# Delta rule of a streaming encoder layer: order of two gram products, of two masks, and the place of one row factor

## The chip, the cores and the metric

One core of one Trainium2 chip runs the whole kernel, one program from the first load to the last store. The metric is the device time of one execution in microseconds. The profile comes from one execution that was recorded on its own; its span reaches from the first to the last instruction.

## The reference, cut to what matters

One encoder layer over 2048 tokens: an input projection with a short convolution, then two groups of heads side by side (four heads of a gated delta rule, four heads of latent attention), an output projection, a feed-forward part and a per-layer embedding gate, all in float32. Only the delta rule is touched here. It works in chunks of 64 tokens:

```python
def gated_delta_rule(q, k, v, g, beta):
    ...
    decay = jnp.exp(jnp.where(tri_incl, g[..., :, None] - g[..., None, :], -jnp.inf))
    k_beta = k * beta[..., None]
    lower = jnp.where(tri_strict, jnp.einsum('nbhid,nbhjd->nbhij', k_beta, k) * decay, 0.0)
    rhs = jnp.concatenate([v * beta[..., None], k_beta * jnp.exp(g)[..., None]], -1)
    sol = lax.linalg.triangular_solve(lower + jnp.eye(CHUNK, dtype=f32), rhs,
                                      left_side=True, lower=True, unit_diagonal=True)
    u, w = sol[..., :DV], sol[..., DV:]
    attn = jnp.where(tri_incl, jnp.einsum('nbhid,nbhjd->nbhij', q, k) * decay, 0.0)
    ...
```

A scan over the chunks then carries a 128x128 state per head: `v_new = u - w S`, `o = q S + attn v_new`, `S = S exp(gl) + k^T v_new`. So `L` (called `lower` above) is the strictly lower part of the gram product of k with k, times the decay, times a factor per row (beta and the square of k's norm factor); `attn` is the gram product of q with k, times the same decay, kept up to the diagonal.

## The kernel before, in words

The function `delta_rule` treats 16 tiles of 128 tokens (two chunks each), all four heads of a tile in one [128, 4, 128] array. Each engine has its own program, and the programs meet in semaphores. They all walk through the same 19 rounds (`steps`): round r prepares tile m = r, forms the inverse's diagonal blocks of tile e = r-1, solves tile n = r-2 and advances the state with tile t = r-3. The order inside a round is written out by hand on each engine, and each engine takes its instructions strictly in that order.

**TensorE (PE)**, in a full round: `a_ws(t,0)` (L1180, w times the state), `s_z(n,0)` (transposes of U at L1151, products with L at L1153), `a_out` (L1096), `a_kv(t,0)` (L1187), `p_turn(m)` (transposes of k and q into the PSUM banks b1 and b0), `a_ws(t,1)`, `a_o(t,0)` (L1196, L1198), `s_y(n,0)` (L1160), `a_kv(t,1)`, `p_turn_v(m)` (ends with the cumulative sums into b3, L1126), `s_z(n,1)`, `a_o(t,1)`, `s_y(n,1)`, `p_gram_k(m)` (k with k into b0, L1132), `s_wu(n)` (w and u from the solved U, L1169 and L1171), `p_gram_q(m)` (k with q into b3, L1138). `p_gram_q` waits for ScalarE to have read b3 (`eg_done`, `dif_done`). Both gram products share one signal, `gram_done`, raised by the last matmul of `p_gram_q`.

**GpSimd (POOL)**, in a full round: `sums(m)` (L1031, the input of the cumulative sums), `substitute(e)` (L1039, then 28 small steps at L1047 and L1049 that invert the 16x16 blocks of L), `decayed(m)` (L1064, q times its decay), then `masks(m)`: decay times the mask up to the diagonal into `dec[:, 1]` (L1054), decay times the mask below it into `dec[:, 0]` (L1056), and that once more times the row factor `made[..., 2]` (L1059).

**VectorE (DVE)** ends a round with `s_u(n,1)` (L1462), `p_lower(m)` (L1434: L = b0 times `dec[:, 0]`, one instruction for the four heads), `p_attention(m)` (L1439: b3 times `dec[:, 1]`), `spread(e)` (L1449, puts the inverted blocks into U, which `s_z(e,0)` of the next round needs) and `a_norm(t)`. The state update `a_s` (L1480) stands earlier in the round: four instructions, one per head, each with a per-row or per-head scalar and a PSUM operand.

**ScalarE (ACT)** squares k and q, makes the decays (`eg` L1284, `dif` L1287 and L1290), copies T (L1304), scales v, squares the output, and copies w and u out of PSUM (`s_copy_wu`, L1311 and L1312). From round 16 on it also splits pieces of attention's first head (`head_high`, L1332 to L1343).

**SyncE (SP)** issues all the stage's transfers from one queue, per round: the inverted blocks to scratch memory (L968), the load of q, k, v for tile e+3 (L917), after the first has landed the blocks back in another layout (`u_blk`, L977), then after `L_done` the store of L (L980), after it has landed the four loads of its diagonal blocks (`blk`, L987), then the output's store and the load of z.

So tile m's L goes through memory to `substitute(m)` on GpSimd in the next round, and GpSimd masks the following tile only behind it.

Of the kernel before, what the change touches and what calls it, by code (L numbers as in the profile page):

```python
# [787 lines left out]
def delta_rule(nc, hT, a_log, dt_bias, norm_g, mixT, blocks_L, blocks_U, latent, at):  # L788
# [10 lines left out]
    with ExitStack() as ctx:  # L799
# [70 lines left out]
        masked = s.sem("masked")  # L870
        gram_done = s.sem("gram_done")
        L_done, attn_done = s.sem("L_done"), s.sem("attn_done")
# [41 lines left out]
        def _(sp):  # L914
# [36 lines left out]
            for r, (m, e, n, t) in enumerate(steps()):  # L951
                if r == TILES:
                    sp.wait_ge(gram_done, TILES)
                    sp.wait_ge(qd_done, TILES)
                    sp.wait_ge(turned_done, TILES)
                    sp.wait_ge(masked, 3 * TILES)
                    sp.wait_ge(L_done, TILES)
                    sp.wait_ge(attn_done, TILES)
                    for rows in (slice(0, ROPE), slice(ROPE, P)):
                        sp.dma_start(raw_kr[rows], latent["krT"]).then_inc(at.kr_loaded, 16)  # L960
                    for piece in range(5):
                        load_head(piece)
# [32 lines left out]
        def _(pool):  # L995
# [55 lines left out]
            def masks(m):  # L1051
                pool.wait_ge(dec_done, m + 1)
                reached(pool, attn_done, m)
                pool.tensor_tensor(dec[:, 1], dif[:, m % 2], each(upto[:]), ALU.mult).then_inc(masked, 1)  # L1054
                reached(pool, L_done, m)
                pool.tensor_tensor(dec[:, 0], dif[:, m % 2], each(below[:]), ALU.mult).then_inc(masked, 1)  # L1056
                pool.wait_ge(masked, 3 * m + 2)
                pool.wait_ge(made_done, 3 * (m + 1))
                pool.tensor_tensor(dec[:, 0], dec[:, 0], heads(made[:, m % 2, 2]), ALU.mult).then_inc(masked, 1)  # L1059

# [10 lines left out]
            for m, e, n, t in steps():  # L1071
                if m is not None:
                    sums(m)
                if e is not None:
                    substitute(e)
                if m is not None:
                    decayed(m)
                    masks(m)
            pool.wait_ge(at.kr_done, 2)
# [13 lines left out]
        def _(pe):  # L1093
# [35 lines left out]
            def p_gram_k(m):  # L1129
                pe.wait_ge(ssq_done, m + 1)  # L1130
                for h in range(HEADS):
                    pe.matmul(b0[:, h], qkv[:, m % 3, HEADS + h], qkv[:, m % 3, HEADS + h], start=True, stop=True)  # L1132

# [75 lines left out]
            for m, e, n, t in steps():  # L1209
# [26 lines left out]
                if first:  # L1236
                    p_gram_k(m)
                if solve:
                    s_wu(n)
                if first:  # L1240
                    p_gram_q(m)
            a_out(TILES - 1)

        @block.scalar
        def _(act):
# [35 lines left out]
            def p_decays(m):  # L1281
                act.wait_ge(turned_done, m + 1)
                reached(act, s_done, 2 * (m - 3) + 1)
                act.activation(eg[:, m % 4], b3[:], ACT.Exp).then_inc(eg_done, 1)  # L1284
                reached(act, masked, 3 * (m - 1))
                for h in range(HEADS):
# [82 lines left out]
        def _(dve):  # L1369
# [38 lines left out]
            def p_factors(m):  # L1408
# [3 lines left out]
                reached(dve, vb_done, m - 1)  # L1412
                reached(dve, masked, 3 * (m - 1))
                dve.tensor_tensor(to[:, 0], rk, rk, ALU.mult).then_inc(made_done, 1)
# [13 lines left out]
            def p_lower(m):  # L1428
                dve.wait_ge(gram_done, m + 1)
                dve.wait_ge(masked, 3 * m + 3)  # L1430
                reached(dve, L_stored, 16 * (m - 2))
                for g in range(2):
                    reached(dve, zp_done[g], NL * (m - 2))
                dve.tensor_tensor(L[:, m % 3], b0[:], dec[:, 0], ALU.mult).then_inc(L_done, 1)  # L1434

            def p_attention(m):
                dve.wait_ge(gram_done, m + 1)
                reached(dve, o_done, 2 * (m - 3))
                dve.tensor_tensor(attnT[:, m % 4], b3[:], dec[:, 1], ALU.mult).then_inc(attn_done, 1)  # L1439
# [1442 lines left out]
```

## Time and profile before

| what | value |
|---|---|
| median of 3 runs | 3335.11 us (3326.7 to 3336.2) |
| the profiled execution, its own time | 3328.85 us |
| its span, first to last instruction | 3327.4 us |
| granted TensorE clock, mean | 0.964 of full speed |
| PE busy | 3072.8 us, 92% of the span |
| DVE, ACT, POOL busy | 1593.7, 1075.9, 1077.9 us |
| the delta rule's stage | from about 666 us to about 1070 us of the span |

The profiled execution lies 6.3 us below the median of the runs, and 1.5 us of its time lie outside its span. A row of the timeline gives the start (us from the start of the span), the duration, engine, line, operation, output and inputs, how many instructions were merged, and in square brackets the idle time in front of it with what ended it. A matmul of 128 columns in float32 shows as two records, so eight records are four matmuls, one per head. SPq is SyncE's queue of transfers: its rows show when a transfer was issued, not when it landed.

### The profile page before, as it was taken

To read this page: it belongs to the slowest core of one execution; us is meant where nothing else is said; L and a number is where in the kernel's file an instruction comes from. 1 tells how busy PE (TensorE), PEld (TensorE's weight loads), DVE (VectorE), ACT (ScalarE), POOL (GpSimd) and SP (SyncE) were. 2 spreads that over 40 slices of the span, in tenths; PEclk is the share of its full clock that TensorE was granted. 3 is DMA by queue.
4 is the path that set the end of the run, shared out by engine and by line. 5 is a ranking of instruction groups with operands and counts; after the bars stand their busy time and mean duration, and the time that the engine had idled before them with its cause. 6 is when DMAs were issued, how large, how long until landed. Compare 5 with 4: busy or idle time off the path is not lost. (4 is left out here: it accounts for less than half of the span.)

```text
span 3327.4 us, 44247 instructions
## 1 busy us (share of the span) xinstructions
PE 3072.8 (92%) x15074; PEld 2540.9 (76%) x15074; DVE 1593.7 (48%) x2713; ACT 1075.9 (32%) x2399; POOL 1077.9 (32%) x1209
## 2 busy tenths in 40 slices
PE   6999997959998899989979999899998999999898
PEld 5888885648786788878768888788887788887686
DVE  3554004535664555556585455865555433233433
ACT  2211004334544555542243333433333211111321
POOL 2222241066665766410073333543331000000122
PEclk9999998979998999999989999999999999999999
DMA  3212115422324211125723222232223333233443
GB/s 136 88 75 77 76 57 168 156 76 67 82 72 107 59 52 53 67 77 178 239 69 122 91 76 83 69 117 93 77 79 110 132 98 101 91 95 117 154 123 99
DMA packets 284414, 329.18 MB, mean 99 GB/s; under 512 B 33281, under 2 KB 224641, under 8 KB 279937
## 3 DMA queue, kind: packets, MB, share of 16 engines
q1 hardware_dynamic: 238632, 265.84, 25.1%
q0 software_dynamic: 12384, 45.09, 3.8%
q10 hardware_dynamic: 33280, 16.78, 1.8%
q8 instruction: 62, 1.02, 0.1%
q14 instruction: 56, 0.45, 0.0%
HBM read 210.73 MB, written 116.92 MB: 98 GB/s over the span
## 5 line engine op out<-in xcount | busy, mean ns | idle before, releaser
L2074 PE MATMUL ff_bank<-ff_x_hi,ff_w_lo 128*128 128x512 f32 x1240 | 487.6, 393 | 31.7 <-DVE ff_w_lo L2254 22.2
L2075 PE MATMUL ff_bank<-ff_x_lo,ff_w_hi 128*128 128x512 f32 x1240 | 486.5, 392 | 0.0
L2076 PE MATMUL ff_bank<-ff_x_hi,ff_w_hi 128*128 128x512 f32 x1240 | 486.3, 392 | 0.0
L2057 POOL TENSOR_TENSOR ff_w_sum<-ff_w_raw 128x512 f32<-128x512 f32 x210 | 301.2, 1444 | 492.4 <-DVE ff_w_lo L2254 434.0
L296 PE MATMUL in_h_ps<-in_x_hi,in_w_lo 128*128 128x512 f32 x704 | 277.5, 394 | 25.7 <-POOL in_w_lo L252 25.7
L2074 PEld LDWEIGHTS ff_bank<-ff_x_hi,ff_w_lo 128*128 128x128 f32 x1240 | 235.4, 190 | 84.0 <-DVE ff_w_lo L2254 25.0
L2464 PE MATMUL fd_acc<-fd_w_hi,fd_a_lo 128*128 128x512 f32 x704 | 279.2, 397 | 11.5 <-DVE fd_a_lo L2448 11.5
L2466 PE MATMUL fd_acc<-fd_w_hi,fd_a_hi 128*128 128x512 f32 x704 | 280.4, 398 | 0.0
L2465 PE MATMUL fd_acc<-fd_w_lo,fd_a_hi 128*128 128x512 f32 x704 | 278.4, 395 | 0.0
L297 PE MATMUL in_h_ps<-in_x_lo,in_w_hi 128*128 128x512 f32 x704 | 276.8, 393 | 0.0
L298 PE MATMUL in_h_ps<-in_x_hi,in_w_hi 128*128 128x512 f32 x704 | 276.4, 393 | 0.0
L2076 PEld LDWEIGHTS ff_bank<-ff_x_hi,ff_w_hi 128*128 128x128 f32 x1240 | 235.1, 190 | 49.4
L2075 PEld LDWEIGHTS ff_bank<-ff_x_lo,ff_w_hi 128*128 128x128 f32 x1240 | 235.3, 190 | 48.8
L2153 ACT ACTIVATE ff_w_hi<-ff_w_sum 128x512 fp32r<-128x512 f32 x210 | 132.5, 631 | 286.9 <-PE ff_bank L2076 264.8
L2448 DVE TENSOR_TENSOR fd_a_lo<-fd_a_raw,fd_a_hi 128x256 fp32r<-128x256 f32 x176 | 74.5, 424 | 287.6 <-ACT fd_a_hi L2438 287.6
L2438 ACT ACTIVATE fd_a_hi<-fd_a_raw 128x256 fp32r<-128x256 f32 x176 | 73.3, 417 | 362.9 <-PE fd_acc L2466 357.3
L1652 POOL TENSOR_TENSOR at_prob<-at_prob,at_scale 128x1536 f32<-128x1536 f32 (+4 forms) x112 | 133.5, 1223 | 139.8 <-DVE at_scale L1836 133.6
L296 PEld LDWEIGHTS in_h_ps<-in_x_hi,in_w_lo 128*128 128x128 f32 x704 | 134.0, 190 | 54.5 <-issue 17.1
L2543 POOL DMA_DIRECT2D scratch_x<-fd_w_raw x16 | 8.5, 534 | 512.3 <-DVE fd_w_raw L2644 512.3
L2464 PEld LDWEIGHTS fd_acc<-fd_w_hi,fd_a_lo 128*128 128x128 f32 x704 | 132.6, 188 | 44.6 <-DVE fd_w_lo L2445 10.7
L2465 PEld LDWEIGHTS fd_acc<-fd_w_lo,fd_a_hi 128*128 128x128 f32 x704 | 132.7, 188 | 32.9
L2466 PEld LDWEIGHTS fd_acc<-fd_w_hi,fd_a_hi 128*128 128x128 f32 x704 | 132.6, 188 | 31.1
(381 smaller groups left out, 6558.5 us busy)
## 6 DMA issues: line engine op xcount, KB each, us to landing
ff_w_raw<-w_gate_up SPq DMA_DIRECT2D x44, 1024.0 KB, 5.2
scratch_hT<-in_out SPq DMA_DIRECT2D x22, 1024.0 KB, 3.9
fd_a_raw<-scratch_hid SPq DMA_DIRECT2D x176, 128.0 KB, 2.1
dr_qkv<-scratch_hT SPq DMA_DIRECT2D x16, 768.0 KB, 5.1
in_w_raw<-w_in POOLq DMA_DIRECT2D x22, 512.0 KB, 3.9
scratch_hid<-ff_first SPq DMA_DIRECT2D x44, 256.0 KB, 2.3
scratch_hid<-ff_second SPq DMA_DIRECT2D x44, 256.0 KB, 2.3
fd_w_raw<-w_down SPq DMA_DIRECT2D x22, 512.0 KB, 5.0
```

The source lines that it names most:

```text
L296: pe.matmul(acc, w_lo[:, b, ws], x_hi[:, k, ts], start=(k == 0), stop=False)
L297: pe.matmul(acc, w_hi[:, b, ws], x_lo[:, k, ts], start=False, stop=False)
L298: last = pe.matmul(acc, w_hi[:, b, ws], x_hi[:, k, ts], start=False, stop=(k == KD - 1))
L1652: last = pool.tensor_tensor(view, view, by, ALU.mult)
L2057: pool.tensor_tensor(w_sum[:, SUM_SLOT[m]], w_raw[:, b, one], w_raw[:, b, two], op).then_inc(w_sum_done, 1)
L2074: pe.matmul(acc, w_lo[:, wm, ws], x_hi[:, xm, k], start=first_mm, stop=False, skip_group_check=skip)
L2075: pe.matmul(acc, w_hi[:, wm, ws], x_lo[:, xm, k], start=False, stop=False, skip_group_check=skip)
L2076: return pe.matmul(acc, w_hi[:, wm, ws], x_hi[:, xm, k], start=False, stop=last_mm, skip_group_check=skip)
L2153: act.activation(w_hi[:, m], src, ACT.Copy).then_inc(w_hi_done, 1)
L2464: pe.matmul(to, self.a_lo[:, slot, rows], self.w_hi[:, k, cols], start=(k == k0), stop=False)
L2465: pe.matmul(to, self.a_hi[:, slot, rows], self.w_lo[:, k, cols], start=False, stop=False)
L2466: last = pe.matmul(to, self.a_hi[:, slot, rows], self.w_hi[:, k, cols], start=False, stop=(k == k1))
```

## The change

It does four things. `p_gram_q` moves on TensorE in front of `s_wu`, directly behind `p_gram_k`, and `p_gram_k` gets a signal of its own (`gram_k_done`). GpSimd does `masks` before `decayed`, within `masks` the one below the diagonal first, and no longer multiplies by the row factor. VectorE's `p_lower` waits for `gram_k_done` and the first mask alone, and brings in the row factor itself, with one instruction per head in the place of one for all four. The counts of `masked` change from three to two per tile, and the wait in `p_factors` that kept `made` from being overwritten under GpSimd goes.

```diff
@@ SyncE, before attention's first loads
-                    sp.wait_ge(masked, 3 * TILES)
+                    sp.wait_ge(masked, 2 * TILES)
@@ GpSimd
             def masks(m):
                 pool.wait_ge(dec_done, m + 1)
+                reached(pool, L_done, m)
+                pool.tensor_tensor(dec[:, 0], dif[:, m % 2], each(below[:]), ALU.mult).then_inc(masked, 1)
                 reached(pool, attn_done, m)
                 pool.tensor_tensor(dec[:, 1], dif[:, m % 2], each(upto[:]), ALU.mult).then_inc(masked, 1)
-                reached(pool, L_done, m)
-                pool.tensor_tensor(dec[:, 0], dif[:, m % 2], each(below[:]), ALU.mult).then_inc(masked, 1)
-                pool.wait_ge(masked, 3 * m + 2)
-                pool.wait_ge(made_done, 3 * (m + 1))
-                pool.tensor_tensor(dec[:, 0], dec[:, 0], heads(made[:, m % 2, 2]), ALU.mult).then_inc(masked, 1)
...
                 if m is not None:
+                    masks(m)
                     decayed(m)
-                    masks(m)
@@ TensorE
                 for h in range(HEADS):
-                    pe.matmul(b0[:, h], qkv[:, m % 3, HEADS + h], qkv[:, m % 3, HEADS + h], start=True, stop=True)
+                    last = pe.matmul(b0[:, h], qkv[:, m % 3, HEADS + h], qkv[:, m % 3, HEADS + h], start=True, stop=True)
+                last.then_inc(gram_k_done, 1)
...
                 if first:
                     p_gram_k(m)
+                    p_gram_q(m)
                 if solve:
                     s_wu(n)
-                if first:
-                    p_gram_q(m)
@@ ScalarE
-                reached(act, masked, 3 * (m - 1))
+                reached(act, masked, 2 * (m - 1))
@@ VectorE
                 reached(dve, vb_done, m - 1)
-                reached(dve, masked, 3 * (m - 1))
...
             def p_lower(m):
-                dve.wait_ge(gram_done, m + 1)
-                dve.wait_ge(masked, 3 * m + 3)
+                dve.wait_ge(gram_k_done, m + 1)
+                dve.wait_ge(masked, 2 * m + 1)
...
-                dve.tensor_tensor(L[:, m % 3], b0[:], dec[:, 0], ALU.mult).then_inc(L_done, 1)
+                for h in range(HEADS):
+                    op = dve.scalar_tensor_tensor(L[:, m % 3, h], b0[:, h], made[:, m % 2, 2, h:h + 1], dec[:, 0, h],
+                                                  ALU.mult, ALU.mult)
+                op.then_inc(L_done, 1)
 
             def p_attention(m):
                 dve.wait_ge(gram_done, m + 1)
+                dve.wait_ge(masked, 2 * m + 2)
```

## Rows read from the trace of the kernel before

**Rows 1.** The page's first part: busy time, share of the span, instructions by engine.
```profile
PE 3072.8 (92%) x15074; PEld 2540.9 (76%) x15074; DVE 1593.7 (48%) x2713; ACT 1075.9 (32%) x2399; POOL 1077.9 (32%) x1209
```

**Rows 2.** Windows between `p_gram_q` starts: length, busy PE, PEld, DVE, ACT, POOL, clock, DMA.
```profile
751.30:771.95 20.65, 19.49 (x157) 16.92 (x155) 13.10 (x38) 10.45 (x46) 11.24 (x32) 1.00 0.12 29
...
815.51:840.04 24.53, 22.50 (x156) 19.60 (x155) 13.76 (x38) 10.49 (x47) 16.95 (x37) 0.86 0.35 95
...
860.69:881.48 20.79, 19.50 (x157) 16.92 (x156) 12.88 (x38) 10.50 (x47) 13.95 (x35) 1.00 0.29 77
...
sum 258.88, PE 239.83 PEld 208.53 DVE 157.25 ACT 125.90 POOL 166.56; mean PE 19.99 PEld 17.38 DVE 13.10 ACT 10.49 POOL 13.88
```

**Rows 3.** Timeline of PE, one round's end, 858 to 864 us.
```profile
858.01 1.06 PE L1132 MATMUL dr_b<-dr_qkv 128*128 128x128 f32 x8
858.90 0.61 PE L1169 MATMUL dr_b<-dr_U,dr_kbg 128*128 128x128 f32 x4
...
860.69 1.06 PE L1138 MATMUL dr_b<-dr_qkv 128*128 128x128 f32 x8
861.68 1.09 PE L1180 MATMUL dr_b<-dr_S,dr_wT 128*64 128x128 f32 x8
863.87 0.44 PE L1151 MATMUL dr_b<-dr_ident,dr_U 128*128 128x128 f32 x2 [1.10 <-DVE dr_U L1449]
```

**Rows 4.** Timeline of POOL in the same round, from the end of `substitute` on.
```profile
857.00 1.26 POOL L1064 TENSOR_TENSOR dr_qdT<-dr_qkv,dr_eg 128x512 f32<-128x512 f32 x1
...
859.46 1.25 POOL L1056 TENSOR_TENSOR dr_dec<-dr_dif,dr_below 128x512 f32<-128x512 f32 x1
860.79 1.04 POOL L1059 TENSOR_TENSOR dr_dec<-dr_dec,dr_made 128x512 f32<-128x512 f32 x1
...
867.39 0.84 POOL L1039 TENSOR_TENSOR dr_inv<-dr_ident_b,dr_blk 32x256 f32<-32x256 f32 x1 [4.55 <-DMA dr_blk<-scratch_blocks_L]
```

**Rows 5.** Timeline of DVE, 852 to 864 us.
```profile
852.32 1.12 DVE L1480 SCALAR_TENSOR_TENSOR dr_S<-dr_S,dr_eg,dr_b 128x128 f32<-128x128 f32 x4 [0.67 <-PE dr_b L1187]
...
861.92 0.69 DVE L1434 TENSOR_TENSOR dr_L<-dr_b,dr_dec 128x512 f32<-128x512 f32 x1 [3.29 <-POOL dr_dec L1059]
...
863.13 0.68 DVE L1449 TENSOR_TENSOR dr_U<-dr_u_blk,dr_diag 128x512 f32<-128x512 f32 x1
```

**Rows 6.** Timeline of SP's queue in the same round.
```profile
857.51 0.37 SPq L917 DMA_DIRECT2D dr_qkv<-scratch_hT  x1
858.55 0.36 SPq L977 DMA_DIRECT2D dr_u_blk<-scratch_blocks_U  x1
862.64 0.34 SPq L980 DMA_DIRECT2D scratch_blocks_L<-dr_L  x1
```

**Rows 7.** DMA view of the stage: transfers by line, KB each, median us to landing.
```profile
dr_qkv<-scratch_hT SPq DMA_DIRECT2D x16, 768.0 KB, 5.1
...
scratch_blocks_L<-dr_L SPq DMA_DIRECT2D x16, 256.0 KB, 2.0
...
dr_u_blk<-scratch_blocks_U SPq DMA_DIRECT2D x16, 32.0 KB, 4.2
```

**Rows 8.** Timeline of PE, rounds 17 to 18: no gram product stands behind `s_wu`.
```profile
1047.75 0.68 PE L1169 MATMUL dr_b<-dr_U,dr_kbg 128*128 128x128 f32 x4 [0.16 <-DVE dr_U L1462]
...
1049.80 1.37 PE L1180 MATMUL dr_b<-dr_S,dr_wT 128*64 128x128 f32 x8
1051.11 0.66 PE L1096 MATMUL dr_b<-dr_ident,dr_on 128*128 128x128 f32 x4
```

**Rows 9.** Timeline of PE, the start of `s_z` in rounds 3, 7 and 17.
```profile
730.71 0.69 PE L1151 MATMUL dr_b<-dr_ident,dr_U 128*128 128x128 f32 x2 [4.93 <-DVE dr_U L1449]
...
819.55 0.44 PE L1151 MATMUL dr_b<-dr_ident,dr_U 128*128 128x128 f32 x2 [1.96 <-DVE dr_U L1449]
...
1032.34 0.69 PE L1151 MATMUL dr_b<-dr_ident,dr_U 128*128 128x128 f32 x2 [1.75 <-DVE dr_U L1449]
```

**Rows 10.** Timeline of ACT in round 17: the copy of T behind attention's pieces.
```profile
1034.70 0.89 ACT L1304 ACTIVATE dr_T<-dr_b 128x256 f32<-128x256 f32 x2
```

More of the change, by code:

```diff
@@ L870, in delta_rule @@
         masked = s.sem("masked")
-        gram_done = s.sem("gram_done")
+        gram_k_done, gram_done = s.sem("gram_k_done"), s.sem("gram_done")
         L_done, attn_done = s.sem("L_done"), s.sem("attn_done")
```

## Prediction, made before the changed kernel ran

> **What bounds the kernel now.** PE is busy 92% of the span [rows 1], but this is a mean over stages; only the delta rule's stage changes, so I read that stage alone, first by windows from one `p_gram_q` to the next [rows 2]. Tiles 3 to 15 are twelve such rounds in 258.88 us, 21.57 us each. The undisturbed ones last 20.65 us and hold 19.49 us of PE work, so PE idles only 1.16 us in them. Three of the twelve are longer with a granted clock under 1.00; the worst is the one of 24.53 us at 0.86, with 22.50 us of PE.
>
> Next the timelines, for who holds whom. PE's last idle time in a round ends on DVE's `spread` [rows 3], which in DVE's order stands behind L and attention. L waits 3.29 us for POOL's row factor [rows 5], which is POOL's fourth operation after the substitution [rows 4]. L is stored 0.03 us after it is made [rows 6], and the substitution of the next round starts at 867.39, 4.78 us after L's end at 862.61 [rows 4, 5]. So there is a **loop**: substitution (10.4 us: the next one ends about 877.75, the one before started 20.77 us before the 867.39) – three masks and q's decay (4.8 us) – L (0.7 us) – memory (4.8 us), 20.7 us together. PE's own round has a floor of 20.65 us in today's order, since L needs `gram_done` from the last product of the round. Two loops of nearly equal length take turns, and where both are late PE waits near 2 us, as the 1.96 us ahead of the slowest round's `s_z` [rows 9].
>
> **The change part by part.** I count time E from the substitution's end (857.00 in the round shown) and G from `p_gram_k`'s start (858.01).
>
> *POOL.* Before L it now has one mask, 1.26 us, in the place of four operations up to 861.83, that is 4.83 us [rows 4]. The row factor's 1.04 us go; q's decay, the mask up to the diagonal and the next `sums` (3.5 us) fall into the 4.78 us in which POOL waits for memory. Cost nothing, cover 4.8 us plus L; if that cover went, 3.5 us would return to the loop.
>
> *DVE.* L becomes four `scalar_tensor_tensor` of 128x128 with one PSUM operand. No row shows exactly these operands. Nearest is the state update, same form and size: 1.12 us for four, against 0.69 us for today's single one [rows 5]. I take +0.43 us; the lower bound is 0, the upper +0.7 (four separate 0.34 us). In POOL's loop this counts in full.
>
> *POOL's loop, new:* 10.4 + 1.26 + 0.1 + 1.12 + 4.78 = 17.7 us, if L's transfer takes what it takes today.
>
> *PE.* `p_gram_q` (0.99 us) goes ahead of `s_wu`. Its two waits are on ScalarE work that ended before the first gram product: today `p_gram_k` to `a_ws` runs without a gap. What was behind it is now uncovered: `a_ws` needs w and u copied, and these copies used to run under `p_gram_q`. Rounds 17 to 18 show that order: from the start of `s_wu` to the end of `a_ws` 1051.11 - 1047.75 = 3.36 us [rows 8]. Today the same work takes 858.90 to 862.77 (863.87 less the 1.10 idle) less 0.99, 2.88 us [rows 3]; 0.07 us of the difference is its first load. So **+0.41 us** per round. Bounds: 0 and 0.6.
>
> *The wait for `spread`.* In G: the gram products end at 1.88, L starts about 1.05 and ends 2.17, attention 2.85, `spread` 3.5; `a_ws` ends 0.99 + 0.89 + 3.29 = 5.2 and `s_z` finds U ready. The 0.96 us that even a PE-bound round idles here (20.65 less 19.49, less 0.2 that the state update causes) go. `spread` also needs `u_blk`, which lands about 5.1 to 5.7 after E (issued 1.55 after it, median 4.2 to landing) [rows 6, 7]; with POOL's loop ahead, E lies near G - 2.8, so it lands at 2.9, in time. Next late is nothing outside PE: the round becomes 20.65 - 0.96 + 0.41 = **20.10 us**, and POOL's 17.7 follows it. Twelve rounds: 258.88 - 241.2 = **17.7 us**. Some 6 us of these are the slowed matmuls of three rounds (PE busy 239.83 against 12 x 19.49 = 233.9 [rows 2]); the slowest of them begins with that wait of 1.96 us [rows 9], and I take it that without such waits the clock stays at 2.4 GHz.
>
> *The fill.* Up to round 3 the POOL loop alone decides (4.93 us of idle PE [rows 9]). Round 0: L moves by 4.83 - 1.0 (no q decay in front there) less 1.26 and 0.43, about 1.9 us. In round 1 one is tempted to take 3.1 us more, but L's store is then issued 2.5 us after E, and the 768 KB load of q, k, v was issued 0.5 us after E and needs 5.1 us [rows 6, 7]. The row that shows what happens to a transfer behind it is `u_blk`: 32 KB, 4.2 us, while L's 256 KB with nothing in front take 2.0 us [rows 7]. So L's store lands about E + 6.3 instead of E + 7.7: 1.35 us. `spread` in round 2 comes 1.0 us sooner after its E (it now waits for `u_blk`, not for L). 1.9 + 1.35 + 1.0 = **4.2 us**. By the Trainium skill (DMA: Bandwidth & Descriptors, "Two DMAs through the same engine are not ordered"), descriptors of one queue on one DMA engine begin in order though they may finish otherwise. That agrees with the 4.2 us. Without such an order the fill would give some 6 us.
>
> *The drain.* Round 16 opens with the gain at `s_z` of 0.96 - 0.41, 0.5 us. In round 17 PE waited 1.75 us for `spread` [rows 9]; this goes, but T's copy starts at 1034.70 only, behind attention's pieces on ACT [rows 10], and the state update stands behind Z in DVE's order. I take 1.0 us.
>
> **Sum.** 4.2 + 17.7 + 0.5 + 1.0 = 23.4 us off 3328.85 (the profiled execution's own time), 3305.4. The median of the runs lies 6.3 us higher; against it I give **3312 us**.
>
> **The rivals.**
>
> *A. PE's round is not the only bound; less comes.* If `u_blk` (behind the load) or L's store slips, L's wait persists in part. L's store is now issued G + 2.2, about E + 5.0, just as the load and `u_blk` clear. Two more us there and POOL's loop is 19.7, still under PE; 3 more and it is 20.7. Then the rounds give 12 x (21.57 - 20.7) = 10, with the rest 13 us: 3322. If only the slowed matmuls are saved, 6 + 4, 3325. For: the 4.2 us of [rows 7]. Against: 2.4 us of slack. Chance 0.20.
>
> *B. More comes.* If the copies hide after all (no 0.41), 12 x 0.41 = 5 us more, and if round 3 no longer starts at the low clock (its idle time shrinks from 4.9 to about 3.4), 3 us more: 3304. For: matmuls at L1151 take 0.69 us there against 0.44 [rows 3, 9]. Against: rows 8 show the copies uncovered. Chance 0.17.
>
> *C. Slower.* L's store collides with the load in every round. From L's end to the substitution's start 4.78 us pass, 2.0 of them the store [rows 4, 5, 7], so with a store of x us POOL's loop is 15.7 + x. It decides against today's 21.57 when x passes 5.9 us. At x = 7, as when it queued behind the whole load and its own reading, the round is 22.7: 12 x 1.1 = 14 us slower less the fill's 4, 3345. Against: PE holds L back to E + 5, when the load has landed. Chance 0.04.
>
> *D. It does nothing.* The stage ends on attention's pieces on POOL and ACT instead of on the rounds, so that the rounds' gain is waited away. Against: those pieces stand behind the last rounds' ACT work and shift with it. 3335. Chance 0.04.
>
> **How the numbers follow.** Forecast 0.55. A measurement of this kernel can tell about 0.3% from no change, 10 us: faster means below 3325. Faster: 0.54 of the forecast, B's 0.17 and 0.09 of A, 0.80. Same: 0.01 of the forecast, 0.10 of A, D's 0.04, 0.15. Slower: C's 0.04 and 0.01 of A, 0.05. The bounds of the unknown costs (0 to 0.7 on L, harmless with 2.4 us of slack; 0 to 0.6 on PE, +5 to -2 us; 0 to 3 us of clock in round 3) carry the forecast from 3303 to 3318. The range takes in most of A and B: 3300 to 3325.
>
> **What the profile after would show.** Right: windows between `p_gram_k` starts near 20.1 us with clock 1.00 in all; no idle time before L1151 ended by `spread` in full rounds; about 0.2 us before `a_ws` and again inside it; L's four instructions start within 0.2 us of `p_gram_k`'s end and take 1.1 us; POOL waits for `blk` and then again for ACT's decays (L1290) before its first mask. Wrong: DVE's L still waiting for `dec` in full rounds (A or C: then look at the store of L's landing, 2.0 us before); rounds of 19.7 (B); a clock under 1.00 in the middle rounds; a stage that starts attention as late as before (D).

## Result and profile after the change

| | before | changed |
|---|---|---|
| median of runs | 3324.6 us (7 runs, 3321.8 to 3336.2) | 3310.57 us (7 runs, 3303.6 to 3314.5) |
| ratio, 95% interval | | 0.9946 [0.9928, 0.9964] |
| the profiled execution | 3328.85 us | 3312.63 us |
| its span, mean granted clock | 3327.4 us, 0.964 | 3311.2 us, 0.964 |

The change is faster by more than the 0.3% named in the prediction: by the ratio some 18 us, by the two medians 14, by the two profiled executions 16.2. The median shown ahead of the prediction, 3335.11, was that of three runs; the four later runs of the same kernel lie between 3321.8 and 3324.6. The forecast of 23.4 us off 3335 is a ratio of 0.993, at the favourable end of the interval. That the forecast time of 3312 us lies only 1.4 us from the measured 3310.57 is luck: the base was 10.5 us too high, and the gain, by the medians, 9.4 us too large.

I read the stage in the same pieces as before. The windows of the changed kernel, cut at the starts of `p_gram_q` from tile 3 on (length, busy PE, PEld, DVE, ACT, POOL, clock, DMA share, GB/s), answer to [rows 2]:

```profile
743.70:763.55 19.85, 19.49 (x156) 16.86 (x155) 13.55 (x41) 10.49 (x48) 12.95 (x34) 1.00 0.12 33
...
823.23:843.87 20.64, 19.75 (x157) 16.89 (x155) 13.53 (x41) 10.50 (x48) 12.94 (x34) 1.00 0.32 83
843.87:864.59 20.72, 19.74 (x156) 16.89 (x155) 13.36 (x41) 10.49 (x48) 13.88 (x35) 1.00 0.32 88
864.59:884.45 19.86, 19.54 (x156) 16.87 (x155) 13.42 (x41) 10.49 (x48) 12.93 (x34) 1.00 0.33 89
...
sum 240.41, PE 235.16 PEld 202.50 DVE 162.51 ACT 125.91 POOL 155.34; mean PE 19.60 PEld 16.87 DVE 13.54 ACT 10.49 POOL 12.94
```

Twelve rounds now take 240.4 us where they took 258.9, none has a clock under 1.00, and PE is busy 235.2 us of them where it was busy 239.8: 4.7 us of the 18.5, mostly matmuls that no longer run at half rate; the rest is idle time of PE. Nine rounds last 19.85 to 19.97 us, one 20.20 and two over 20.6.

The stage in three pieces, from DVE's first clearing of S to attention's first score product:

| piece | before | changed | difference | forecast |
|---|---|---|---|---|
| start to `p_gram_k` of tile 3 (fill) | 82.31 | 78.51 | -3.8 | -4.2 |
| `p_gram_k` of tile 3 to that of tile 15 | 258.88 | 240.42 | -18.5 | -17.7 |
| from there to attention (drain) | 63.13 | 69.95 | **+6.8** | -1.5 |
| whole stage | 404.32 | 388.88 | -15.4 | -23.4 |

(The stage also began 2.0 us sooner in this profile and what follows it took 1.2 us longer; both lie outside the edit.) Two pieces come out as worked out, against this one profile of the kernel before. A second profile of the same rounds exists: `e8_before_pieces_behind_t`, described below, is the kernel before with an edit that lies behind them. Its twelve rounds take 255.0 us, so the rounds' gain is 18.5 by one profile and 14.6 by the other. The third piece has the other sign, and the experiments had to explain it.

The timeline of PE in the changed kernel shows the new order and the price of the copies, beside [rows 3]:

```profile
863.70 1.06 PE L1129 MATMUL dr_b<-dr_qkv 128*128 128x128 f32 x8
864.59 1.06 PE L1136 MATMUL dr_b<-dr_qkv 128*128 128x128 f32 x8
865.49 0.61 PE L1167 MATMUL dr_b<-dr_U,dr_kbg 128*128 128x128 f32 x4
...
867.46 1.37 PE L1178 MATMUL dr_b<-dr_S,dr_wT 128*64 128x128 f32 x8
868.77 0.44 PE L1149 MATMUL dr_b<-dr_ident,dr_U 128*128 128x128 f32 x2
```

Both gram products stand together, and from the start of `s_wu` (L1167) to the end of `a_ws` (L1178) pass 3.28 us. The `s_z` behind it has no idle time in brackets: U was ready.

The timeline of DVE in two rounds of the changed kernel answers to [rows 5]:

```profile
848.03 0.69 DVE L1449 TENSOR_TENSOR dr_U<-dr_u_blk,dr_diag 128x512 f32<-128x512 f32 x1 [2.23 <-DMA dr_u_blk<-scratch_blocks_U]
...
884.65 1.13 DVE L1431 SCALAR_TENSOR_TENSOR dr_L<-dr_b,dr_made,dr_dec 128x128 f32<-128x128 f32 x4 [0.47 <-PE dr_b L1129]
885.70 0.68 DVE L1439 TENSOR_TENSOR dr_attnT<-dr_b,dr_dec 128x512 f32<-128x512 f32 x1
887.26 0.69 DVE L1449 TENSOR_TENSOR dr_U<-dr_u_blk,dr_diag 128x512 f32<-128x512 f32 x1 [0.89 <-DMA dr_u_blk<-scratch_blocks_U]
```

L now waits for its gram product (0.47 us of idle DVE) and no longer 3.29 us for POOL. `spread` (L1449), which I had expected to find its block landed, waits for it in ten of the twelve rounds, 0.6 to 2.2 us. Most of this wait is covered, since PE comes for U later than that; at 2.1 and 2.2 us it is not, and these are the two rounds over 20.6 us, in which PE idles 0.57 and 0.66 us ahead of `s_z`.

The timeline of POOL in the changed kernel, from the end of one substitution to the start of the next, answers to [rows 4]:

```profile
881.67 1.27 POOL L1054 TENSOR_TENSOR dr_dec<-dr_dif,dr_below 128x512 f32<-128x512 f32 x1
882.89 1.28 POOL L1056 TENSOR_TENSOR dr_dec<-dr_dif,dr_upto 128x512 f32<-128x512 f32 x1
884.13 1.28 POOL L1061 TENSOR_TENSOR dr_qdT<-dr_qkv,dr_eg 128x512 f32<-128x512 f32 x1
885.35 1.05 POOL L1031 TENSOR_TENSOR dr_cums<-dr_upto,dr_scal 128x512 f32<-128x512 f32 x1
891.72 0.84 POOL L1039 TENSOR_TENSOR dr_inv<-dr_ident_b,dr_blk 32x256 f32<-32x256 f32 x1 [5.32 <-DMA dr_blk<-scratch_blocks_L]
```

The mask that L needs ends at 882.94, before L's product does; the other three operations lie in the time in which POOL would wait for memory, and 5.32 us of waiting are left over. POOL no longer sets the pace. One term of its loop grew, though: from L's end to the start of the next substitution 4.7 to 7.1 us pass in the twelve rounds, where it was 4.8 to 5.7 before; in the round shown it is 891.72 - 885.78 = 5.94.

### The profile page after: what moved, and what is told of

It reads as the page before. It is cut to its first block and busy times, and to the rows that moved or that the text cites. A ratio compares the mean times of both kernels' runs of the same rounds, so it can differ in the third digit from the quotient of the medians.

```text
span 3311.2 us, 44267 instructions
## 1 busy us (share of the span) xinstructions
PE 3075.2 (93%) x15074; PEld 2541.1 (77%) x15074; DVE 1600.0 (48%) x2761; ACT 1075.6 (32%) x2399; POOL 1061.2 (32%) x1193
```

## Experiments

Every time is the median of its runs, every ratio is against runs of the kernel before on the same chip. "Rounds" is the sum of the twelve windows, "drain" the third piece of the table above.

**The changed kernel twice more**, unaltered, on two chips.

> The changed kernel, unaltered, once more, as the yardstick for the others. Theory T (two loops set the rounds; the drain gives some 7 us back through a late T copy on ScalarE and low clock behind it): 0.9946 of before within 0.003; the twelve windows between second gram products sum to 240 to 243 us; in round 17 PE idles 2.7 us before its second w-times-state product and the clock is at 1.2 GHz behind it. Rival R (the low clock of the drain is chance, not a wait): round 17 shows the same order of work, but PE at 2.4 GHz, and the stage is 6 to 8 us shorter than the 388.9 us of the first profile.

> The changed kernel a third time, beside the others on the same chip. Windows 240 to 243 us; ratio 0.993 to 0.996; the drain 66 to 70 us if its low clock has a cause in the order of work (a wait of 2 to 2.8 us before the second w-times-state product of round 17), 62 to 64 in this draw if it is chance.

Measured: 3311.81 us, 0.9944 [0.9921, 0.9966], and 3307.57 us, 0.9941 [0.9921, 0.996]. Fill 78.5 and 78.6, rounds 240.7 and 239.8: all but the same. The drain is not: 67.4 us in one and 61.1 in the other, after 70.0 in the first profile. The timeline of PE in the drain, first profile of the changed kernel:

```profile
1005.91 0.44 PE L1149 MATMUL dr_b<-dr_ident,dr_U 128*128 128x128 f32 x2 [0.39 <-DVE dr_U L1449]
...
1011.87 0.76 PE L1178 MATMUL dr_b<-dr_S,dr_wT 128*64 128x128 f32 x5 [2.75 <-DVE dr_S L1480]
...
1026.11 0.68 PE L1167 MATMUL dr_b<-dr_U,dr_kbg 128*128 128x128 f32 x4 [0.16 <-DVE dr_U L1462]
...
1032.68 0.76 PE L1178 MATMUL dr_b<-dr_S,dr_wT 128*64 128x128 f32 x5 [1.22 <-DVE dr_S L1480]
...
1047.39 1.11 PE L1093 MATMUL dr_b<-dr_ident,dr_on 128*128 128x128 f32 x4 [4.83 <-DVE dr_on L1496]
```

and the same rows in the third profile (`c2_change_third`):

```profile
1007.56 0.44 PE L1149 MATMUL dr_b<-dr_ident,dr_U 128*128 128x128 f32 x2 [1.47 <-DVE dr_U L1449]
...
1012.44 0.76 PE L1178 MATMUL dr_b<-dr_S,dr_wT 128*64 128x128 f32 x5 [1.67 <-DVE dr_S L1480]
...
1021.96 0.68 PE L1167 MATMUL dr_b<-dr_U,dr_kbg 128*128 128x128 f32 x4 [0.16 <-DVE dr_U L1462]
...
1028.53 0.76 PE L1178 MATMUL dr_b<-dr_S,dr_wT 128*64 128x128 f32 x5 [1.22 <-DVE dr_S L1480]
...
1039.07 1.12 PE L1093 MATMUL dr_b<-dr_ident,dr_on 128*128 128x128 f32 x4 [4.83 <-DVE dr_on L1496]
```

Round 17's two waits sum to 3.14 us in both (0.39 + 2.75, 1.47 + 1.67; in the second profile 1.05 + 2.08). The same work from the state update to the next `s_wu` then takes 14.24 us in one and 9.52 in the other, and the last stretch 14.71 and 10.54. These 4.7 and 4.2 us are the whole 8.9 between the drains, and the windows view over ten of these microseconds says what they are. In the first profile:

```profile
1012.00:1022.00 10.00, 10.00 (x52) 8.89 (x51) 3.83 (x9) 0.98 (x3) 7.61 (x6) 0.55 0.76 203
```

The same window in the third profile, `c2_change_third`:

```profile
1012.00:1022.00 10.00, 9.41 (x77) 8.20 (x77) 5.22 (x14) 3.16 (x11) 8.19 (x6) 1.00 0.90 245
```

At a granted clock of 0.55 PE gets through 52 matmuls in the time in which it gets through 77 at 1.00. So the +6.8 us of the drain is TensorE at 1.2 GHz, in some executions of one and the same program and not in others; with 2.4 GHz through rounds 17 and 18 the drain is 61.1 us, 2.0 less than before.

**TensorE's order alone**, on the kernel before:

```diff
                 if first:
                     p_gram_k(m)
+                    p_gram_q(m)
                 if solve:
                     s_wu(n)
-                if first:
-                    p_gram_q(m)
```

> The kernel before with one edit: the k-with-q product ahead of w and u on TensorE. GpSimd and VectorE as before. Theory T: L gets its gram product 1.8 us sooner but still waits for GpSimd's row factor, so GpSimd's loop of 20.7 us sets every round: windows near 20.75 us, sum 248 to 251 against 258.9 before and 240.4 after; time 6 to 10 us below before (ratio 0.997 to 0.998). Rival (TensorE's order alone is what paid): sum 240 to 243, ratio 0.995.

Measured: 3328.89 us, 1.0001 [0.9991, 1.0012]; rounds 262.0. By itself the new order brings nothing. Windows of this kernel:

```profile
809.36:837.15 27.79, 23.82 (x157) 20.65 (x156) 13.97 (x38) 10.61 (x48) 18.62 (x41) 0.82 0.34 92
```

and its PE timeline inside that window:

```profile
817.37 0.69 PE L1151 MATMUL dr_b<-dr_ident,dr_U 128*128 128x128 f32 x2 [3.77 <-DVE dr_U L1448]
817.85 1.06 PE L1153 MATMUL dr_b<-dr_U,dr_L 128*128 128x128 f32 x4
```

PE can now do a round in 19.85 us while POOL's loop still needs 20.7. PE runs ahead for three rounds (19.85, 20.15, 20.82), is then held 3.77 us (3.88 and 2.84 the next two times), and its products behind that wait take 1.06 us for four, where they take 0.61 at full clock. That costs what the order gives. My expected 248 to 251 us had no place for this: an engine that is faster than its supplier pays the difference in lumps, and the lumps are long enough to go with a lower clock.

**GpSimd's and VectorE's part alone**: the changed kernel with `p_gram_q` put back behind `s_wu`, the diff above the other way round.

> The changed kernel with the k-with-q product put back behind w and u on TensorE; GpSimd, VectorE and the separate signal stay. Theory T: L comes early and GpSimd's loop is short, but attention and behind it spread wait for the last product, so TensorE idles 0.96 us before each round's solve: windows 20.65 us, sum 247 to 250; time 8 to 13 us below before (ratio 0.996 to 0.9975). Rival (GpSimd's loop alone is what paid): sum 240 to 243, ratio 0.995.

Measured: 3309.6 us, 0.994 [0.9924, 0.9957], no different from the whole change. Every round lasts 20.05 us, not the 20.65 that I expected, and they sum to 240.6. PE's timeline has the reason:

```profile
863.78 0.44 PE L1149 MATMUL dr_b<-dr_ident,dr_U 128*128 128x128 f32 x2 [0.37 <-DVE dr_U L1450]
```

The wait ahead of `s_z` shrinks from 0.96 to 0.37 us. I had taken it to go only with the product's move, because attention and `spread` stand behind `gram_done`. But `spread` stood behind L too, and L, with `gram_k_done` of its own, is now made under `s_wu`; only attention's 0.69 us still come between the last product and `spread`. So moving the product is worth 0.2 us a round in the quiet rounds (20.05 against 19.86), 2.3 us in twelve, and the three long rounds give it back: nothing that the profiles of the rounds or the times can tell. Its drain, 73.6 us, is longer than any of the changed kernel's: in round 17 PE waits 2.64 us for `spread`, and some 15 us at 1.2 GHz follow. The gain is in POOL's order, L's own signal, or both.

**The row factor back on POOL**, directly behind the mask below the diagonal, L again a single operation, the rest of the change kept:

```diff
+                pool.tensor_tensor(dec[:, 0], dec[:, 0], heads(made[:, m % 2, 2]), ALU.mult).then_inc(masked, 1)
...
-                for h in range(HEADS):
-                    op = dve.scalar_tensor_tensor(L[:, m % 3, h], b0[:, h], made[:, m % 2, 2, h:h + 1], dec[:, 0, h],
-                                                  ALU.mult, ALU.mult)
-                op.then_inc(L_done, 1)
+                dve.tensor_tensor(L[:, m % 3], b0[:], dec[:, 0], ALU.mult).then_inc(L_done, 1)
```

> The changed kernel with the row factor back on GpSimd, right behind the mask below the diagonal (L is again one VectorE instruction for four heads). Theory T: GpSimd's loop grows from 17.7 to 18.4 us, still under TensorE's 19.85, so the windows stay at 19.85 to 20.2 us, sum 240 to 243; only the fill loses 0.6 us in each of its rounds, 2 us in all; ratio to before 0.994 to 0.996. Rival (the row factor's move carried the gain): windows above 20.5 us, sum over 246.

> The changed kernel with the row factor on GpSimd, unaltered, once more. Theory T: its windows sum to 238 to 241 us again; its ratio is that of the changed kernel within the interval (0.993 to 0.996), since the drain of 62.5 us in its first profile was one draw of 62 to 70. Rival (its drain is short for a reason): drain again under 64 us and ratio under 0.9935.

Measured: 3306.12 us, 0.9937 [0.9921, 0.9954], and again 3303.80, 0.9938 [0.9916, 0.996]; rounds 238.4 and 238.6, drain 62.5 and 62.4. It is as fast as the change, perhaps 4 to 6 us faster, which the intervals can't tell. The full rounds have slack for POOL's 1.04 us; moving them to DVE brings nothing there. In both profiles the rounds are even 1.2 to 2.4 us shorter than in the three of the change, with no wait of PE ahead of `s_z` in a full round; why was not tested. The fill, 78.8 and 78.6 us against 78.5, lost 0.1 to 0.3 us and not the 2 that I expected. The product's move and the factor's move can each be taken back alone without loss; both at once was not tried. What is left to carry the gain is that the mask for L comes first on POOL and that L has a signal of its own.

**Attention's first pieces behind T's copy** in the drain, because in the first profile ACT spends 1004.85 to 1009.64 on them while the copy of T, Z and the state update wait behind:

```diff
-        HIGH_AT = {(TILES, "wu"): (0, 2), (TILES + 1, "t"): (2, 5), (TILES + 1, "wu"): (5, 11), (TILES + 2, "end"): (11, PIECES)}
+        HIGH_AT = {(TILES + 1, "t"): (0, 5), (TILES + 1, "wu"): (5, 11), (TILES + 2, "end"): (11, PIECES)}
...
-                if (r, place) == (TILES, "wu"):
+                if (r, place) == (TILES + 1, "t"):
```

> The changed kernel with ScalarE's splitting of attention's rope key and first two pieces moved from the end of round 16 to behind round 17's copies of T. Theory T (the late T copy holds Z, and behind it the state update in VectorE's order; the low clock follows that wait): TensorE's idle time before the second w-times-state product of round 17 falls from 2.75 to 1.2 us, the clock stays at 2.4 GHz until the last round, and from the last k-with-k product to attention's first matmul it takes 61 to 64 us instead of 70.0 and 67.4; time 4 to 7 us below the changed kernel (ratio to before 0.992 to 0.9935). Rival (the low clock of the drain comes of itself, or of the 1.2 us waits that are in every drain round): the wait shrinks, the clock still falls, the drain stays over 66 us.

> The kernel before with the move of attention's pieces alone. Theory T: there TensorE waited 1.75 us for spread in round 17 while ScalarE worked on the pieces, so the late T copy was half hidden; PE still waits for spread and for 1.2 us of state update, drain 61 to 63 us against 63.1, time within 2 us of before (ratio 0.9985 to 1.0005). Rival (the pieces' place costs the same whatever stands in front): 5 us and more below before.

Measured on the changed kernel: 3310.22 us, 0.9947 [0.9927, 0.9968], drain 66.6; on the kernel before: 3330.49 us, 1.0004 [0.9987, 1.0022], drain 75.4. The wait of 2.75 us fell to 1.22 as intended, and the clock stayed at 1.00 behind it. But a wait of 2.02 us appeared later, and the last 20 us ran at 1.2 GHz instead. DVE, POOL and PE in the timeline of `e3_pieces_behind_t`:

```profile
1019.86 1.27 POOL L1087 TENSOR_TENSOR at_v_lo<-dr_qkv,at_v_hi 128x512 fp32r<-128x512 f32 x1
1020.15 1.00 DVE L1486 TENSOR_TENSOR dr_orn<-dr_orn 128x4 f32<-128x4 f32 x1 [0.59 <-ACT dr_orn L1323]
...
1021.21 1.27 POOL L1087 TENSOR_TENSOR at_q_lo<-dr_qkv,at_q_hi 128x512 fp32r<-128x512 f32 x1
1021.26 1.23 DVE L1489 TENSOR_TENSOR dr_orn<-dr_orn,dr_ossq 128x4 f32<-128x4 f32 x1
...
1024.56 0.67 DVE L1471 TENSOR_TENSOR dr_vnew<-dr_u,dr_b 64x512 f32<-64x512 f32 x1
1024.70 0.66 PE L1093 MATMUL dr_b<-dr_ident,dr_on 128*128 128x128 f32 x4 [2.02 <-DVE dr_on L1496]
```

DVE's operations of four columns take 1.00 and 1.23 us there (a third, 1.20), where they take 0.15 or 0.16 in other rounds. The pieces, moved later, put POOL's work beside them. On the kernel before, the moved pieces change nothing in the time; its profile has a wait of 3.15 us ahead of round 17's `s_z` and nearly 20 us at 1.2 GHz behind it. The expectation that the drain would become 61 to 64 us failed both times: one wait is taken away and another takes its place.

**`u_blk` ahead of the load.** SP issues the 32 KB transfer that `spread` waits for before the 768 KB load of q, k, v and not behind it:

```diff
+                    sp.dma_start(u_blk[:, e % 2], src).then_inc(u_loaded[e % 2], 16)
                     if e + 3 < TILES:
...
                         load(e + 3)
-                    sp.dma_start(u_blk[:, e % 2], src).then_inc(u_loaded[e % 2], 16)
```

(The two waits in front of that transfer go with it.)

> The changed kernel with SyncE's order turned round: the inverted blocks come back (u_blk) before the 768 KB load of q, k, v is issued. Theory T: u_blk lands 2 us after its issue and not 4 to 5, spread waits for no transfer in full rounds, and the rounds of 20.6 to 20.7 become 19.85: twelve windows sum to 238 to 239 instead of 240.4 to 240.7. The load is issued 1.5 us later, L's store behind it lands a microsecond later, which GpSimd's slack covers. Time 1 to 3 us below the changed kernel. Rival (the load now delays L's store so much that GpSimd's loop passes 19.85 us): L waits for GpSimd's mask in full rounds and the windows are over 20.5 us.

Measured: 3323.74 us, 0.999 [0.9975, 1.0004]: most of the change's gain is gone, and the rival of the expectation came true. Rounds 255.5, 21.3 us each on average, five of the twelve between 21.1 and 21.5. The timeline of one round of this kernel, rows of DVE, SP's queue and POOL:

```profile
934.69 1.13 DVE L1431 SCALAR_TENSOR_TENSOR dr_L<-dr_b,dr_made,dr_dec 128x128 f32<-128x128 f32 x4 [1.70 <-POOL dr_dec L1054]
...
936.89 1.72 DVE L1449 TENSOR_TENSOR dr_U<-dr_u_blk,dr_diag 128x512 f32<-128x512 f32 x1 [0.28 <-DMA dr_u_blk<-scratch_blocks_U]
...
934.88 0.36 SPq L972 DMA_DIRECT2D dr_u_blk<-scratch_blocks_U  x1
935.35 0.45 SPq L917 DMA_DIRECT2D dr_qkv<-scratch_hT  x1
935.85 0.74 SPq L980 DMA_DIRECT2D scratch_blocks_L<-dr_L  x1
...
944.27 0.84 POOL L1039 TENSOR_TENSOR dr_inv<-dr_ident_b,dr_blk 32x256 f32<-32x256 f32 x1 [6.22 <-DMA dr_blk<-scratch_blocks_L]
```

The row of L's store in this kernel's DMA view of the twelve rounds (count, KB, median us from issue to landing):

```profile
scratch_blocks_L<-dr_L SPq DMA_DIRECT2D x12, 256.0 KB, 5.7
```

`u_blk` lands in 1.9 us, as wished. But the load now starts 1.5 us later, 0.5 us ahead of L's store, and the store needs 5.7 us where it needs 2.5 in the changed kernel and 2.0 before. This is rival C of the prediction, brought about from another side, and its formula gives the average round: 15.7 + 5.7 = 21.4 us. L waits for POOL again (1.70 us) and the loop of memory and GpSimd sets the pace. `spread`, now early enough to stand beside POOL's operations, takes 1.1 to 1.9 us in these rounds instead of 0.69. The Trainium skill (DMA: Bandwidth & Descriptors, "Two DMAs through the same engine are not ordered") has descriptors of one queue on one DMA engine start in order: the two transfers that stand behind the load in these kernels agree, the 32 KB with 4.3 us against 1.9 and the 256 KB with 5.7 against 2.0.

**Both of the last two edits together, attention's pieces behind T's copy and `u_blk` ahead of the load.**

> The changed kernel with both edits, attention's pieces behind the T copies and u_blk ahead of the load. Theory T: the two add up, rounds 238 to 239 us and drain 61 to 64 us, stage 378 to 381 us; time 6 to 9 us below the changed kernel, ratio to before 0.991 to 0.993. Rival: as for the two alone.

Measured: 3325.16 us, 0.9993 [0.9982, 1.0003]; rounds 259.2, drain 67.9. A miss; it repeats what each did, the 2.02 us wait late in the drain included.

**The load behind everything that is waited for.** The experiments leave one place for the 768 KB, whose data is not used until tile e + 3 is prepared: after L's store and the four loads of `blk`.

```diff
-                    if e + 3 < TILES:
-                        sp.wait_ge(gram_done, e + 1)
-                        sp.wait_ge(qd_done, e + 1)
-                        sp.wait_ge(turned_done, e + 1)
-                        load(e + 3)
...
                         sp.dma_start(blk[h * NB:(h + 1) * NB, m % 2], src).then_inc(blk_loaded[m % 2], 16)
+                if e is not None and e + 3 < TILES:
+                    sp.wait_ge(gram_done, e + 1)
+                    sp.wait_ge(qd_done, e + 1)
+                    sp.wait_ge(turned_done, e + 1)
+                    load(e + 3)
```

> The changed kernel with the 768 KB load of q, k, v moved behind the loads of L's diagonal blocks on SyncE, so that neither u_blk nor L's store stands behind it. Theory T (what is left in the changed kernel's rounds is the load in front of u_blk and L's store): u_blk lands in 2 us, L's store in 2.0, spread waits for no transfer, all twelve windows are 19.85 us (sum 238.2); in the fill L's store no longer waits for the load, another 2 to 3 us; up to the last k-with-k product 4 to 6 us less than the changed kernel. Whole time 2 to 6 us below the changed kernel, ratio to before 0.993 to 0.9945, blurred by the drain, which takes 62 to 70 us from run to run. Rival (the load, now late, holds something else, the output's store, the load of z or its own tile): windows over 20 us or a wait for q, k, v at the transposes.

> The kernel before with the same move of the load. Theory T: there L's store was issued 5 us behind the load and landed in 2.0 us anyway, and spread waited for L, not for u_blk, so nothing moves: twelve windows 253 to 261 us as in the profiles of that order, ratio 0.998 to 1.001. Rival (the load's place is worth something by itself): 4 us and more below before.

Measured on the changed kernel: **3300.98 us** (6 runs, 3298.2 to 3303.1), 0.9919 [0.9901, 0.9937]. The unaltered change beside it took 3307.57 (3302.7 to 3310.8), so this version is some 7 us faster than it (2 to 6 were expected), the best of both kernels and all variants. Its windows are even, and the wait of `spread` for its block is gone from the full rounds:

```profile
sum 238.27, PE 234.41 PEld 202.32 DVE 163.70 ACT 125.93 POOL 155.57; mean PE 19.53 PEld 16.86 DVE 13.64 ACT 10.49 POOL 12.96
```

All twelve last 19.85 or 19.86 us, and from L's end to the next substitution it is 4.7 to 5.4 us again. The fill is 75.0 us, 3.5 less than the change's: round 3's wait of PE, 4.93 us before [rows 9] and 3.71 with the change, is 1.55 here. L's store lands in 2.0 us, `u_blk` in 1.9, and the load itself in 5.6, which nobody waits for. On the kernel before, the same edit measured 3326.44 us, 1.0 [0.9986, 1.0014]: there L started only 4.9 us after the substitution, and its store was issued as the load landed. The edit pays here only once POOL's order is changed.

## Why the prediction was right, and which step failed

The loop through POOL, L and memory was the right mechanism for the rounds and for the fill. The time of 3312 us came out so near by luck, by two errors that cancel. I took the 6.3 us by which the three runs' median lay above the profiled execution as lasting; the median of seven runs lies 4.3 us below it. And of the 23.4 us forecast some 18 came by the ratio, 14 by the medians.

- **POOL's loop: right.** L no longer waits for POOL, the three displaced operations are covered, with 5.3 us to spare in the round shown. Putting the loop back to 15.7 + 5.7 us by way of the store (`e6_ublk_before_load`) brought back rounds of 21.3 us and nearly the old time, so that loop bounds the rounds when it is longer than PE's. The runs say which part of the change shortens it: POOL's order together with L's own signal; the two were not tried apart.
- **L as four operations: right.** 1.13 us against 1.12 from the state update; and hidden, since one operation with the factor on POOL is no slower.
- **The copies of w and u: right.** 3.28 us from `s_wu` to the end of `a_ws`, forecast 3.29, before 2.88.
- **The wait for `spread`: right in outcome, its cause half seen.** 20.10 us was forecast, 19.86 came. The 0.96 us went and the copies cost 0.40, as forecast. What I had no term for: `p_gram_q` directly behind `p_gram_k` takes 0.90 us where it took 0.99 in front of `a_ws`, and in a round that starts `s_z` without a wait the stretch to the next `p_gram_k` is 14.79 us and not 14.93: 20.65 - 0.96 + 0.40 - 0.09 - 0.14 = 19.86. The wait goes mainly because L is ready early, not because the product is moved (20.05 us without the move).
- **`u_blk` in time: wrong, small.** It was to land at G + 2.9 and `spread` to start at G + 2.85. In the round shown `p_gram_k` starts at 883.56 and `spread` at 887.26: G + 3.7. The block landed 5.7 us after E, as worked out; it is E that lies at G - 2.0 and not at G - 2.8, because L's way through memory took 5 to 7 us in the middle rounds and not the 4.78 that "if L's transfer takes what it takes today" had kept. Rival A's mechanism is real, and costs 240.4 - 238.3 = 2.1 us of the rounds. Its size was bounded by the slack that I had counted.
- **The slowed matmuls: right.** The waits went and with them every clock under 1.00 in twelve rounds; PE's busy time fell by 4.7 us, forecast some 6. Some of it depends on the execution compared with: in the second profile of the old order PE was busy 235.3 us, with one round under 1.00.
- **The fill: right.** 3.8 against 4.2. Counted from the start of the stage, round 0's L came 2.0 us sooner (forecast 1.9; the sum as written, with 1.0 for q's decay, gives 2.1, and with the 1.26 of [rows 4] 1.9), the substitution behind round 1's L 1.35 more (1.35), `spread` another 0.4 (1.0), since it waits 2.44 us for `u_blk` there. What I had held back for transfers behind the load was real: moving the load releases 3.5 us more.
- **The drain: the step that failed.** "In round 17 PE waited 1.75 us for `spread`; this goes ... I take 1.0 us." The wait for `spread` went to 0.39 in the first profile (1.05 and 1.47 in the others), and the wait for the state update behind it grew from 1.22 to 2.75: together 3.14 where it had been 2.97. T's copy behind attention's pieces decides both, as the sentence said, and then it left nothing to gain, not 1.0. At full clock the drain still fell by 2.0 us, near the forecast of 1.5, but by another way: 0.8 us through the shorter stretch up to round 17 and 1.3, the longer waits taken off, through matmuls behind the wait that no longer ran slowly. What I had no term for was the clock: two of three profiles of the changed kernel lost 6.3 and 8.9 us to 1.2 GHz in the drain. In the first profile the 8.9 us are more than the whole difference between 16.2 us and 23.4. That it also explains the spread of the runs (11 us for the changed kernel) is likely and was not shown, since only profiled executions have a trace.

What stays open is why equal waits are followed by a long stretch at 1.2 GHz in one execution and by none in another. The split of the wait does not decide it, as the drains of all profiles show (waits of PE in round 17, ahead of `s_z` and of the second `a_ws`):

| run | waits | drain |
|---|---|---|
| before | 1.75 + 1.22 | 63.1 |
| e8 (pieces moved, on before) | 3.15 + 1.22 | 75.4 |
| e11 (load moved, on before) | 1.27 + 1.87 | 65.1 |
| e1 (product moved, on before) | 1.96 + 1.22 | 62.6 |
| changed, three profiles | 0.39 + 2.75, 1.05 + 2.08, 1.47 + 1.67 | 70.0, 67.4, 61.1 |
| e2 (product back) | 2.64 + 1.22 | 73.6 |
| e4, twice | 0 + 3.21, 0.33 + 2.80 | 62.5, 62.4 |
| e6 (`u_blk` first) | 0.57 + 2.56 | 62.4 |
| e9 (load last) | 2.11 + 1.22 | 62.7 |
| e3, e7 (pieces moved) | 0.39 + 1.22, 0.74 + 1.22, each with 2.02 later | 66.6, 67.9 |

`e4_again` had nearly the split of the first profile of the change, and its row of PE

```profile
1009.40 1.33 PE L1181 MATMUL dr_b<-dr_S,dr_wT 128*64 128x128 f32 x5 [2.80 <-DVE dr_S L1481]
```

shows slow matmuls behind the wait as well; but over the ten microseconds from that row on its clock is 0.86, where it is 0.56 in the first profile of the change over the ten from 1011.87 on. The kernel before kept its clock at 1.00 behind one wait of 2.43 us in a full round.

The first of the two waits has a cause that no run here removed. In round 17 `spread` waits for `u_blk` in every profile, 4.12 us before, 2.76 to 3.84 in the changed kernel and still 4.49 with the load of q, k, v moved. What stands ahead in SP's queue there are attention's first loads. In the timeline of the changed kernel:

```profile
994.31 0.51 SPq L949 DMA_DIRECT2D dr_qkv<-scratch_qnT  x1
1000.57 0.33 SPq L968 DMA_DIRECT2D scratch_blocks_U<-dr_inv  x1
1003.29 0.37 SPq L977 DMA_DIRECT2D dr_u_blk<-scratch_blocks_U  x1
```

`u_blk` is issued once the store in front of it has landed: 2.72 us later here and 4.36 in `e9_load_behind_blk`, against 1.48 in the quiet rounds just before. That these loads hold the store up is likely, since the loads issued last before it take 8 us and more to land; it was not tested.

## What to carry to other kernels

Draw the loops that run through several engines and memory, and order each engine's work by what leads back into the loop: the mask that L needs, moved ahead on GpSimd, with a signal of its own for L's product, was in every version that kept the 18 us here; each of the two other parts could be taken back alone without a measurable loss. Then issue the big transfer that nobody waits for behind the small ones that somebody does; its place is worth nothing while another loop is longer, and 7 us once it isn't. A saving in an engine that is not the loop's slowest link came back here as a few long waits; make it together with the link.

## What the runs showed of the hardware that I had not expected

- **The clock can differ between executions of one program.** Same program, same 3.14 us of waiting in round 17, and TensorE ran the next ten microseconds once at 2.4 GHz and twice at 1.2 (0.55 and 0.58 over 1012 to 1022 us). A single profile misjudges the drain by up to 8.9 us.
- **A 32 or 256 KB transfer behind 768 KB in one queue** takes 4.3 us instead of 1.9, and 5.7 instead of 2.0 (`e6_ublk_before_load`; issued 3.5 to 3.8 us behind the load, as in the changed kernel, 2.5).
- **DVE's smallest operations can last as long as POOL's large ones.** 128x4 operations took 1.00 to 1.23 us instead of 0.16, each ending with a POOL operation of 1.27 us, and three of them, one after another, held PE for 2.02 us. A larger one stretches too: `spread` took 1.72 us in the row of `e6_ublk_before_load` above instead of 0.69. It is there in the kernel before as well, in its timeline of POOL and DVE:

```profile
833.65 1.30 POOL L1064 TENSOR_TENSOR dr_qdT<-dr_qkv,dr_eg 128x512 f32<-128x512 f32 x1
833.85 1.12 DVE L1414 TENSOR_TENSOR dr_made<-dr_rn 128x4 f32<-128x4 f32 x1
```

  By the Trainium skill (SBUF — State Buffer, "SBUF: two separate sides") VectorE and GpSimd share one pair of ports, which whoever starts first holds for its whole instruction, and a VectorE operation with both inputs in SBUF needs it beside a GpSimd operation that reads SBUF. The traces agree: the stretched operations have both inputs in SBUF, and L1471, one of whose inputs is in PSUM, kept its 0.67 us beside a POOL operation at 1024.56.
